# Both value projections as one two-step product in 2x2 blocks, with five low parts made by an adding DMA

## What is computed

```python
h = rms_norm(x, norm_mix[l])
proj = jnp.einsum('btd,dn->btn', h, w_in[l])      # 256 x 2048 times 2048 x 11264
q_a, f_a, i_a, g_a, q_b, k_b, v_b, gate_logits = jnp.split(proj, split_pts, axis=-1)
...
y_a = hgrn2_mixer(q_a, f_a, i_a, g_a, ...)        # i_a holds the values (1024 columns)
y_b = chunked_relpos_attention(q_b, k_b, v_b, ...)  # v_b holds the values (1024 columns)
```

## Time and profile before

| | |
|---|---|
| median of three runs | 2129.19 us (2129.09 to 2130.63) |
| profiled execution | 2129.45 us, its span 2127.8 us |
| TensorE granted clock | 0.999 of full |
| PE busy | 2117.2 us, 10098 matmuls |
| DVE busy | 1750.1 us (82%) |
| ACT busy | 1396.1 us (66%) |
| POOL busy | 225.5 us (11%) |
| IV, PE's first matmul to that of AV | 104.88 to about 148.4 us |
| AV, to PE's first matmul of G_IN | about 148.4 to 189.9 us |

### The profile page before, as it was taken

The page is one execution under the profiler, slowest core; times in us unless marked ns, Lnnn a source line. Parts: engine busy times, 40 slices in busy tenths (PEclk is TensorE's granted clock), DMA queues, the critical chain, the costliest instruction groups (busy, mean ns, idle before and its releaser), DMA issues.

```text
span 2127.8 us, 30210 instructions
## 1 busy us (share of the span) xinstructions
PE 2117.2 (99%) x10098; PEld 1775.5 (83%) x10098; DVE 1750.1 (82%) x2295; ACT 1396.1 (66%) x1617; POOL 225.5 (11%) x314
## 2 busy tenths in 40 slices
PE   9999999999999999999999999999999999999998
PEld 9988888888888888888888888888888888888887
DVE  5578788676666699999899898988989999998976
ACT  6465455456545676766767677768778777876665
POOL 2021433201000000000000000000000111110000
PEclk9999999999999999999999999999999999999999
DMA  8566545565555588889888787877788888887664
GB/s 269 180 196 203 157 156 159 181 222 178 179 186 181 187 249 252 254 247 251 258 255 243 230 244 233 237 220 217 226 246 239 245 245 246 233 232 229 201 194 139
DMA packets 225344, 462.76 MB, mean 217 GB/s; under 512 B 14712, under 2 KB 14816, under 8 KB 225120
## 3 DMA queue, kind: packets, MB, share of 16 engines
q1 hardware_dynamic: 208464, 402.31, 57.6%
q0 software_dynamic: 15744, 55.65, 14.9%
q10 hardware_dynamic: 1040, 3.55, 0.5%
HBM read 409.01 MB, written 3.16 MB: 194 GB/s over the span
## 4 chain that ended last, share of the span: by engine, by line
PE 98%; DVE 1%; ACT 0%; issue 0%; DMA 0%; DVEq 0%; SPq 0%; ACTq 0%
PE gp L2149 35%; PE gp L2081 33%; PE mx L2149 13%; PE gp L2172 8%; PE gp L2176 4%; PE mx L2429 1%; PE mx L2313 1%; PE mx L2478 1%; DMA x_tok<-x_in 0%; PE mx L2316 0%; PE mx L2310 0%; PE mx L2365 0%; PE mx L2409 0%; PE mx L2324 0%; PE mx L2353 0%
## 5 line engine op out<-in xcount | busy, mean ns | idle before, releaser
L733 ACT ACTIVATE w_hi<-raw 128x1024 fp32r<-128x1024 f32 x759 | 797.6, 1057 | 543.5 <-PE gp L2081 257.4
L1324 DVE TENSOR_TENSOR w_lo<-raw,w_hi 128x1024 fp32r<-128x1024 f32 x663 | 807.5, 1231 | 237.6 <-ACT w_hi L733 225.2
L2081 PE MATMUL gp<-w_hi,a_hi 128*128 128x512 f32 x576 | 229.9, 399 | 0.0
L2149 PE MATMUL gp<-w_hi,a_hi 128*128 128x512 f32 x585 | 228.0, 390 | 0.0
L2149 PE MATMUL gp<-w_lo,a_hi 128*128 128x512 f32 x585 | 227.7, 389 | 0.0
L2149 PE MATMUL gp<-w_hi,a_lo 128*128 128x512 f32 x585 | 227.6, 389 | 0.0
L2081 PE MATMUL gp<-w_lo,a_hi 128*128 128x512 f32 x576 | 224.6, 390 | 0.0
L2081 PE MATMUL gp<-w_hi,a_lo 128*128 128x512 f32 x576 | 224.2, 389 | 0.0
L681 POOL DMA_DIRECT2D low<-raw x96 | 81.3, 847 | 1229.0 <-ACT low L740 1229.0
L1567 DVE TENSOR_TENSOR t_lo<-t_sum,t_hi 128x1536 fp32r<-128x1536 f32 x102 | 178.9, 1754 | 10.6 <-ACT t_hi L869 7.4
L869 ACT ACTIVATE t_hi<-t_sum 128x1536 fp32r<-128x1536 f32 x102 | 150.9, 1479 | 5.2 <-PE gp L2149 5.2
(11 more groups left out here) (439 smaller groups left out, 4319.3 us busy)
## 6 DMA issues: line engine op xcount, KB each, us to landing
raw<-a_w_in_in SPq DMA_DIRECT2D x192, 512.0 KB, 5.2
raw<-w_ffn_in_in SPq DMA_DIRECT2D x176, 512.0 KB, 5.2
raw<-w_in_in SPq DMA_DIRECT2D x175, 512.0 KB, 3.4
low<-raw POOLq DMA_DIRECT2D x96, 512.0 KB, 6.5
raw<-w_ffn_out_in SPq DMA_DIRECT2D x88, 512.0 KB, 5.5
raw<-a_w_out_in SPq DMA_DIRECT2D x64, 512.0 KB, 3.7
raw<-w_out_in SPq DMA_DIRECT2D x32, 512.0 KB, 3.7
raw<-w_proj_a_in SPq DMA_DIRECT2D x16, 512.0 KB, 3.7
```

Of the source, the lines that this page charges most:

```text
L733: act.activation(w_hi[:, place], raw[:, slot], ACT.Copy).then_inc(hi_ready, 1)
L1324: dve.tensor_tensor(w_lo[:, slot], raw[:, slot], w_hi[:, place], ALU.subtract).then_inc(lo_ready, 1)
L2081: ins = pe.matmul(out_, stat, mov, start=start, stop=last and p == 2, skip_group_check=True)
L2149: ins = pe.matmul(out_, stat[sp_], mov[mp], start=start and p == 0, stop=stop and p == 2, skip_group_check=True)
```

## The change

Segments IV and AV become one segment `VAL` of form "D" with two steps, i_a and then v_b. Step 0 has pairs 4 and 6 by seven products, step 1 has pairs 2, 4 and 6, as AV had. In step 0 the low parts of units 7, 11 and 15 come from the adding DMA, in step 1 those of units 7 and 11. Both values are now read from `cx_part` by ACT. The work of `hgrn_first` is spread over both steps: the clamp moves to place 2, the q product to 6, the first half of the decay table to place 11 of step 0, the second half to place 2 of step 1, the exponentials to place 4 of step 1. On POOL the five adding DMAs are issued ahead of `weigh(0, 0)`. Because an odd number of low parts is added ahead, later ones take the other buffer of the two.

```diff
+MIXED_VAL = ((4, 6), MIXED)
+ADDED_VAL = ((7, 11, 15), (7, 11))
...
-            Segment(w_in, "N", 1, D, (2 * DM, 2 * DM + NB), 2 * NB, a_op),
-            Segment(w_in, "D", 1, D, (6 * DM, 6 * DM + NB), 2 * NB, a_op),
+            Segment(w_in, "D", 2, D, (2 * DM, 2 * DM + NB), 4 * DM, a_op),
...
+            for i in range(S[VAL].steps):          # POOL
+                for unit in added_units(VAL, i):
+                    add_low(VAL, i, unit)
             pool.wait_ge(pre_ready, 2)
             weigh(0, 0)
-            pool.wait_ge(bank_free[1], 1 + block0[IV] // 2 + 1)
+            pool.wait_ge(val_ready, 2)
             head_values(0, 0)
-            pool.wait_ge(val_ready, 2)
+            pool.wait_ge(val_ready, 4)
             load_gate_rows(pool, 0)
...
-                if j == 11:                        # ACT
+
+            def hgrn_second(i, j):
+                if j == 4:
                     decay_exp(0, 0)
...
-            run(IV, val_out, mid=hgrn_first)
-            double_step(AV, 0, second_out, nothing_between)
+            double_step(VAL, 0, val_out, hgrn_first)
+            double_step(VAL, 1, val_out, hgrn_second)
...
-                if j == 3:                         # DVE
+                if j == 2:
                     dve.tensor_scalar(f_a, f_a, LN_MIN, None, ALU.max).then_inc(pre_ready, 1)
-                if j == 5:
+                if j == 6:
                     dve.tensor_tensor(q_a, q_a, wide[:], ALU.mult).then_inc(pre_ready, 1)
+                if j == 11:
                     dve.wait_ge(consts, 1 + MASKED)
                     dve.wait_ge(ln_ready, 1)
                     dve.wait_ge(pre_ready, 2)
-                if j in (7, 8):
-                    decays(0, 0, j - 7)
+                    decays(0, 0, 0)
+
+            def hgrn_second(i, j):
+                if j == 2:
+                    decays(0, 0, 1)
...
-            run(IV, none, mid=hgrn_first)
-            double_step(AV, 0, no_head, no_mid)
-            dve.wait_ge(parts_read, 1)
+            double_step(VAL, 0, no_head, hgrn_first)
+            double_step(VAL, 1, no_head, hgrn_second)
+            dve.wait_ge(parts_read, 2)
...
-            run(IV)                                # PE
-            double_step(AV, 0, nothing_between)
-            pe.wait_ge(parts_added, 1)
+            for i in range(S[VAL].steps):
+                double_step(VAL, i, nothing_between)
+            pe.wait_ge(parts_added, S[VAL].steps)
```

More of the change, by code:

```diff
@@ L376, in build @@
         ]
-        QF, IV, AV, G_IN, QK, GATES, PROJ_A, PROJ_B, OUT, FFN_IN, FFN_OUT, V_IN, UG_IN, Y_FIRST, Y_LAST = range(len(S))
+        QF, VAL, G_IN, QK, GATES, PROJ_A, PROJ_B, OUT, FFN_IN, FFN_OUT, V_IN, UG_IN, Y_FIRST, Y_LAST = range(len(S))
         unit0, block0 = [0], [0]
@@ L419, in t_of @@
         def t_of(k):
-            return tx if k == AV else (t_sum, t_hi, t_lo)
+            return tx if k == VAL else (t_sum, t_hi, t_lo)
         def c_of(k):
-            return cx_part if k == AV else c_part
+            return cx_part if k == VAL else c_part
         WIDE = (FFN_IN, V_IN, UG_IN,)
         def mixed(k, i):
-            if k == AV:
-                return MIXED
+            if k == VAL:
+                return MIXED_VAL[i]
             if k == FFN_OUT:
@@ L441, in build @@
         done_steps, done_pairs = {}, {}
-        for k in (AV, FFN_IN, FFN_OUT, V_IN, UG_IN, Y_FIRST):
+        for k in (VAL, FFN_IN, FFN_OUT, V_IN, UG_IN, Y_FIRST):
             done_steps[k] = sum(S[q].steps for q in done_steps)
@@ L507, in raw_use @@
             return i * (16 * S[k].pair // RAW) + 16 * ((unit0[k] + j) // RAW + 1)
-        BY_DMA = (FFN_IN, FFN_OUT, V_IN, UG_IN)
+        BY_DMA = (VAL, FFN_IN, FFN_OUT, V_IN, UG_IN)
         def added_units(k, i):
+            if k == VAL:
+                return ADDED_VAL[i]
             if k == FFN_OUT:
@@ L646, in head_values, with add_low @@
                 pool.tensor_copy(v_head[:], val[:, which, :, bass.ds(h * DH, DH)]).then_inc(v_ready, 1)
+            made = [0]
+            def add_low(k, i, unit):
+                buf = added(k, i, unit)[0]
+                made[0] += 1
+                pool.wait_ge(neg_ready, made[0])
+                pool.dma_start(low[:, buf].bitcast(F32), raw[:, raw_slot(k, i, unit)], accum_op=ALU.add).then_inc(lo_added[buf], 16)
+            for i in range(S[VAL].steps):
+                for unit in added_units(VAL, i):
+                    add_low(VAL, i, unit)
             pool.wait_ge(pre_ready, 2)
             weigh(0, 0)
-            pool.wait_ge(bank_free[1], 1 + block0[IV] // 2 + 1)
+            pool.wait_ge(val_ready, 2)
             head_values(0, 0)
-            pool.wait_ge(val_ready, 2)
+            pool.wait_ge(val_ready, 4)
             load_gate_rows(pool, 0)
@@ L672, in _ @@
                 head_values(h, 1)
[L674 to L681, removed]
             for i in range(S[FFN_IN].steps):
@@ L895, in double_step, with val_out @@
                         mid(i, j)
[L897 to L903, removed]
+            def val_out(i, half):
                 for t, c in enumerate(((0, 3), (2, 1))[half]):
-                    ins = act.activation(val[:, 1, t, half * NB:(half + 1) * NB], cx_part[:, c], ACT.Copy, scale=rx[:, t:t + 1])
+                    ins = act.activation(val[:, i, t, half * NB:(half + 1) * NB], cx_part[:, c], ACT.Copy, scale=rx[:, t:t + 1])
                 own.link(ins)
@@ L910, in second_out @@
                     act.sem_inc(parts_read, 1)
-            def nothing_between(i, j):
-                pass
-            run(IV, val_out, mid=hgrn_first)
-            double_step(AV, 0, second_out, nothing_between)
+            double_step(VAL, 0, val_out, hgrn_first)
+            double_step(VAL, 1, val_out, hgrn_second)
             def cross_copy(h):
@@ L2220, in shared_banks @@
                         pe.wait_ge(ws_copied, 1)
-                elif k == AV:
+                elif k == VAL:
                     pe.wait_ge(parts_added, dbl(k, i))
@@ L2243, in mixed_pair @@
                 else:
-                    s1_, s2_, s3_, s4_ = [[x_[:, q] for x_ in ((sx_hi[:, n], sx_lo[:, n]) if k == AV else s_of(u // 2))]
+                    s1_, s2_, s3_, s4_ = [[x_[:, q] for x_ in ((sx_hi[:, MIXED.index(u)], sx_lo[:, MIXED.index(u)]) if k == VAL else s_of(u // 2))]
                                           for q in range(4)]
```

## The result

The changed kernel takes 2137.02 us (median of 8 executions, 2135.45 to 2138.06), the kernel before in the same rounds 2129.53 (2129.09 to 2130.69). The ratio is 1.0033, 95% interval 1.0024 to 1.0043: slower by 7.5 us where 0.5 was forecast, and outside the range of 2127.7 to 2132.2. The profiled execution took 2137.9 us, its span 2136.3, 8.5 more than the span of before.

What follows compares the result with a forecast made beforehand. PE, busy 99% of the span, was taken to bound the kernel. Matmuls dropped (-1.36), the wait at the start (+1.12) and the border stall (+0.7) gave +0.5 us: 2129.7 on the median, range 2127.7 to 2132.2.

Steps and rivals of the forecast that it cites:

- Matmuls: Pairs 4 and 6 of the first step lose three matmuls each on PE: -1.36 us.
- Start: At step 0's second unit PE waits for DVE to empty bank 1, last used by QF: +1.12 us.
- Border: Between the steps, DVE's late partial results and bank additions stall PE at step 1's second unit: +0.7 us, bounds 0 and 3.
- Adding DMAs: In both steps the added low parts land before PE wants them: cost 0, at most 0.6 us together.
- POOL beside DVE: Weighing at step 1's last pair slows DVE by 0.94 us, which fits into 4.7 of cover at pair 6.
- the shut-out: Rival: while POOL weighs, DVE stands for 14.09 us less 4.7 of cover, 9.4 slower, 2139.1 us; chance 0.04.

Runs made afterwards that it cites:

- gap_plain: Kernel before, with POOL's first weighing made to wait for DVE's low part of AV's second unit, no DMA ahead; 2129.79 us, ratio 1.0.
- before_dma_ahead: Kernel before, with a plain 128 KB DMA issued by POOL right ahead of the first weighing; 2129.7 us, ratio 1.0001.
- filler: Changed kernel, with a POOL memset, not waited for, between last issue and weighing; five executions took 2129.86 to 2131.36 us, five 2135.66 to 2136.84.
- wait_landing: Changed kernel, with POOL waiting for the last adding DMA's landing ahead of the weighing; 2130.63 us, ratio 1.0005.
- early_wait: Changed kernel, with QF's last bank emptied ahead of the split and POOL waiting for the last adding DMA's landing; 2130.2 us, ratio 1.0005.
- gap_add: Kernel before, with the weighing waiting for DVE's low part of AV's second unit, then behind a 512 KB adding DMA; 2131.11 us, ratio 1.0007.

## Why the prediction was wrong

**Matmuls, -1.36:** right, six fewer.

**Start, +1.12:** right. DVE takes until 109.90 to empty the bank (108.68 + 1.22), and PE resumes at 109.95 after 108.70: 109.95 - 108.70 - 0.23 = 1.02, and 0.11 of restart, 1.13 (the kernel's start-up was 1.31 later in this execution, so the times stand against 107.62 + 1.31). PE's timeline, answering to the earlier trace rows:

```profile
108.70 0.39 PE L2152 MATMUL gp<-w_lo,a_hi 128*128 128x512 f32 x1
109.95 0.50 PE L2152 MATMUL gp<-w_hi,a_hi 128*128 128x512 f32 x1 [0.86 <-DVE qf L1393]
110.29 0.40 PE L2152 MATMUL gp<-w_hi,a_lo 128*128 128x512 f32 x1
```

**Border, +0.7:** right. I had DVE begin the partial results at 143.7; they begin at 145.07, which is 143.76 without the later start-up. The second bank is added by 152.79, and PE stops between 152.08 and 152.85: 0.54, with the restart 0.65. DVE's timeline, answering to the earlier trace rows:

```profile
145.07 0.68 DVE L1574 TENSOR_TENSOR cx_part<-mx,cx_part 128x512 f32<-128x512 f32 x1
...
148.04 1.29 DVE L1604 TENSOR_TENSOR cx_part<-gp,cx_part 128x512 f32<-128x512 f32 x2
149.25 2.35 DVE L1323 TENSOR_TENSOR w_lo<-raw,w_hi 128x1024 fp32r<-128x1024 f32 x2
151.51 1.28 DVE L1604 TENSOR_TENSOR cx_part<-gp,cx_part 128x512 f32<-128x512 f32 x2
```

**Adding DMAs, 0:** right. The five landings (tile `low` in these stages) and no wait of PE on `low`:

```profile
DMA to landing us min/median/max: 6.2/7.0/7.2
```

**POOL beside DVE, hidden:** this is the step that failed. I weighed 0.94 us of delay against 4.7 of cover and gave the shut-out 0.04. In its place DVE was kept out for 8.79 - 1.22 = 7.57 us, of which PE felt 4.04 (so the cover of this subtraction was 3.5; the 4.7 was that of the low part of the sums), and 1.73 more by the restart and the low clock that followed the stop, a term I did not have at all. The argument was a mean: in the earlier trace rows POOL's records fill 14.09 us and DVE is busy for 10.59 of them, from which I took it that POOL bears most of the clash. That held where the two alternate. It said nothing of a case in which POOL keeps its turn; there the weighing needs 178.67 - 171.16 = 7.5 us instead of 14.09, and the subtraction waits for all of it and for the copy behind it. The rival had the right mechanism and was priced from the wrong length: 14.09 less 4.7 gave 9.4, the unbroken run gave 5.8.

The Trainium skill (SBUF — State Buffer, "Who interferes with whom") says that a DVE instruction with two SBUF inputs contends with a GpSimd instruction that reads SBUF, under an exclusive lock, and that issue order decides who blocks. The exclusion the trace bears out: a subtraction of 1.22 us lasted 8.79 while POOL worked. What it does not bear out is a reading by which the wait is one instruction long: here it was eighteen.

**The sum.** From before to changed G_IN begins 197.72 - 190.10 = 7.62 later: -1.36, +1.13, +0.65, +4.04, +1.73 and 1.31 of later start-up make 7.50. The start-up is not the change's: it does the same work in both, and the profiles of other kernels here that don't touch it have 23.54 to 25.57 there (gap_plain, a variant of the kernel before, has 25.57). After G_IN's start the spans differ by another 0.9, of which a wait on `y_one` is 0.6; before_dma_ahead shows one of 0.7 as well, and its cause was not looked for. On the medians the kernels lie 7.49 apart, and the change's own terms, without the start-up, make 6.19; four of the eight executions of the changed kernel took 2135.45 to 2136.16, four, the profiled one among them, 2137.88 to 2138.06, and only the start-up of that one is known. Without the unbroken run the forecast holds: in filler's profile G_IN begins at 190.57, 0.47 after 190.10, where 0.5 was forecast.

**What stays open** is what lets POOL keep its turn for eighteen operations. The long run was seen only where the weighing stood ready behind the adding DMA's issue and, in the profiles, the copy came ahead of DVE's subtraction. With a real wait between the issue and the weighing (a landing in wait_landing and early_wait, a rounding, its own memset) it was gone: of the 41 executions of these four kernels 40 took 2132.61 or less, and the one other took 2645.6, over 500 us more, which nothing here explains. Whether the wait or the copy's later place did it is not separated. Nor is it shown what is enough: in the profiles of the kernel before with an adding DMA ahead the long run is missing, but the one profiled for gap_add is among its three shortest. The source and place of that DMA also differ from those of the changed kernel, and I have no profile of the long run outside it.

## What to carry to other kernels

POOL and DVE did not share evenly here: before moving a long queue of ready POOL operations beside a DVE that feeds PE, price it as one block too, here 7.9 us against 3.5 of cover, and not only by the slowdown seen where they alternate. Where such a queue stood behind a DMA issue, a wait that really held it (POOL's own memset sufficed) took the long run away. When one program gives two times 5.8 us apart, look for an outcome decided by tenths of a microsecond between two engines, and find the stop of that size.

## What the runs showed of the hardware

- POOL kept DVE out for eighteen operations in a row (8.79 us for a subtraction of 1.22), for the rest of a copy and four operations (2.87 for a sum of 0.69, in filler), or took turns with it (1.48 for the same subtraction, in the kernel before at 147.06), with the same operations on POOL.
- Taking turns cost POOL more than DVE: the same weighing takes 14.1 us in the kernel before, 13 to 22 in the variants, and 7.5 unbroken.
- After PE had stood for 4.04 us at a granted clock of 1.00 and resumed, the clock read 0.50 (1.2 GHz) for the three microseconds from 181 to 184. The stops of 1.02 and 0.54 had no such sequel: the matmuls behind the restart stand 0.23 to 0.24 apart, and the granted clock reads 1.00 there.
- A restart cost the first matmul 0.11 (0.34 to the next one), as in the earlier trace rows.
